# Moving the inputs of the long products off multiples of 32 bytes in a one-layer hybrid decoder kernel

## What is computed

```python
x = x + 0.5 * swiglu(rms_norm(x), ffn1_gate, ffn1_up, ffn1_down)    # 1024 -> 2816 -> 1024
h = rms_norm(x); proj = h @ w_in                                    # 1024 -> 5120
y_a = moba_attention(q, k, v, rel_bias)                             # 8 heads of 64
y_b = rwkv7_time_mix(h, r, k, v, ...)                               # 8 heads of 64, with low-rank products of h
merged = sigmoid(ga) * (y_a @ proj_a) + sigmoid(gb) * (y_b @ proj_b)
x = x + merged @ w_out
x = x + 0.5 * swiglu(rms_norm(x), ffn2_gate, ffn2_up, ffn2_down)
out = rms_norm(x)
```

## Time and profile before

| | us |
|---|---|
| median of 3 runs | 625.43 |
| the three runs | 623.08, 625.43, 632.48 |
| the profiled execution's own time | 623.61 |
| its span, first to last instruction | 621.8 |

### The profile page before, as it was taken

How to read it: one execution, slowest core, us unless ns; L and a number is a source line. 1 busy time by engine, 2 the same in 40 slices (tenths; PEclk the granted TensorE clock), 3 DMA queues, 4 the chain that set the end, 5 groups by cost and what they waited for, 6 DMA issues and landing times.

```text
span 621.8 us, 15455 instructions
## 1 busy us (share of the span) xinstructions
PE 611.3 (98%) x6716; PEld 596.6 (96%) x6716; DVE 419.7 (68%) x491; ACT 296.7 (48%) x345; POOL 91.8 (15%) x92
## 2 busy tenths in 40 slices
PE   8999999999999999999999999999999999999996
PEld 8999999999999999999988899999999999999996
DVE  5866887755656369968993337878667666665663
ACT  6644555443334264535555445545544444443332
POOL 0117700000114000020015423004100000000130
PEclk9999999999999999999999999999999999999999
DMA  8677666656555246685242232356556666556551
GB/s 298 213 245 218 198 202 202 194 173 197 176 188 185 76 136 204 203 177 163 71 137 71 71 105 73 122 183 203 161 177 202 202 186 187 188 169 208 179 167 67
DMA packets 100672, 105.40 MB, mean 170 GB/s; under 512 B 2244, under 2 KB 98732, under 8 KB 100628
## 3 DMA queue, kind: packets, MB, share of 16 engines
q1 hardware_dynamic: 99380, 101.47, 51.1%
q0 software_dynamic: 1088, 3.02, 2.2%
q10 hardware_dynamic: 160, 0.27, 0.1%
HBM read 103.50 MB, written 1.25 MB: 168 GB/s over the span
## 4 chain that ended last, share of the span: by engine, by line
PE 86%; DVE 7%; ACT 3%; DMA 3%; issue 1%; SPq 0%; ACTq 0%; DVEq 0%
PE two L1460 24%; PE two L1461 23%; PE two L1462 23%; PE two L1456 12%; DVE w_lo L904 4%; ACT w_hi L532 2%; DMA w_raw<-in_ffn_down 1%; DMA w_raw<-in_ffn_up 1%; DMA w_raw<-in_ffn_gate 1%; DVE w_lo L914 1%; PE two L1734 1%; PE two L1735 1%; PE two L1736 1%; PE two L1879 0%; DVE hlo_f L923 0%
## 5 line engine op out<-in xcount | busy, mean ns | idle before, releaser
L532 ACT ACTIVATE w_hi<-w_raw 128x2048 fp32r<-128x2048 f32 (+1 forms) x86 | 162.5, 1890 | 241.7 <-PE two L1462 207.7
L904 DVE TENSOR_TENSOR w_lo<-w_raw,w_hi 128x2048 fp32r<-128x2048 f32 (+1 forms) x86 | 199.6, 2321 | 82.7 <-ACT w_hi L532 82.4
L1460 PE MATMUL two<-hlo_f,w_hi 128*128 128x256 f32 x640 | 177.7, 278 | 1.4 <-DVE w_lo L904 1.4
L1461 PE MATMUL two<-hhi_f,w_lo 128*128 128x256 f32 x640 | 177.2, 277 | 0.0
L1462 PE MATMUL two<-hhi_f,w_hi 128*128 128x256 f32 x640 | 177.2, 277 | 0.0
L1460 PEld LDWEIGHTS two<-hlo_f,w_hi 128*128 128x128 f32 x640 | 120.3, 188 | 2.4 <-issue 1.3
L1461 PEld LDWEIGHTS two<-hhi_f,w_lo 128*128 128x128 f32 x640 | 120.2, 188 | 0.0
L1462 PEld LDWEIGHTS two<-hhi_f,w_hi 128*128 128x128 f32 x640 | 120.2, 188 | 0.0
L1460 PE MATMUL two<-hid_lo_t,w_hi 128*128 128x256 f32 x352 | 97.9, 278 | 0.9 <-DVE w_lo L904 0.3
L1461 PE MATMUL two<-hid_hi_t,w_lo 128*128 128x256 f32 x352 | 97.4, 277 | 0.0
L1462 PE MATMUL two<-hid_hi_t,w_hi 128*128 128x256 f32 x352 | 97.4, 277 | 0.0
(11 more groups left out here) (342 smaller groups left out, 984.3 us busy)
## 6 DMA issues: line engine op xcount, KB each, us to landing
w_raw<-in_ffn_up SPq DMA_DIRECT2D x21, 1024.0 KB, 5.3
w_raw<-in_ffn_gate SPq DMA_DIRECT2D x20, 1024.0 KB, 5.3
w_raw<-in_w_in SPq DMA_DIRECT2D x20, 1024.0 KB, 5.1
w_raw<-in_ffn_down SPq DMA_DIRECT2D x16, 896.0 KB, 4.6
w_raw<-in_ffn_down SPq DMA_DIRECT2D x8, 1024.0 KB, 4.9
w_raw<-in_w_out SPq DMA_DIRECT2D x4, 1024.0 KB, 4.9
w_raw<-in_proj_a SPq DMA_DIRECT2D x4, 512.0 KB, 3.6
w_raw<-in_proj_b SPq DMA_DIRECT2D x4, 512.0 KB, 4.2
```

The source lines that it names most:

```text
L532: nc.scalar.activation(whi[slot][:, 0:kts], raw[slot][:, 0:kts], ACT.Copy).then_inc(sg["hi_ready"], 1)
L904: nc.vector.tensor_tensor(wlo[slot][:, 0:kts], raw[slot][:, 0:kts], whi[slot][:, 0:kts].bitcast(F32), ALU.subtract).then_inc(sg["lo_ready" ...
L1460: mm(dst, whi[slot][:, k_, cols], xl, start=start, stop=False)
L1461: mm(dst, wlo[slot][:, k_, cols], xh, start=False, stop=False)
```

## The change

The pairs of tiles `hhi_f`/`hlo_f`, `hid_hi_t`/`hid_lo_t`, `hhi_m`/`hlo_m` and `mhi`/`mlo` each become one tile (`pair_f`, `pair_hid`, `pair_m`, `pair_mg`) that is 8 elements longer, of which a view is taken that begins 4, 4, 2 and 6 elements in, that is 16, 16, 8 and 24 bytes behind a multiple of 32. With the pads, the distance to the weights goes from -64 bytes to -48 for the feed-forward input, -80 for the hidden rows, -56 for the mixing's input and -72 for the merged branches. `yahi`, `yalo`, `ybhi`, `yblo` and all weight tiles stay where they were; the mixing's scratch tiles from `ks` on move by 32 bytes and stay at multiples of 32. No instruction of any engine is added, removed or moved against another, and all shapes stay; operands' addresses differ.

```diff
+        def shifted(name, tiles, by, scope):
+
+            flat = sb(name, [P, 2 * tiles * T + 8], F32R, scope)[:, by:by + 2 * tiles * T]
+            both = flat.rearrange("p (a k t) -> p a k t", a=2, k=tiles)
+            return both[:, 0], both[:, 1]
+
         with ExitStack() as sc:
             h_f = sb("h_f", [P, KD, T], scope=sc)
             sb("pad_f", [P, 48], scope=sc)
-            hhi_f = sb("hhi_f", [P, KD, T], F32R, scope=sc)
-            hlo_f = sb("hlo_f", [P, KD, T], F32R, scope=sc)
+            hhi_f, hlo_f = shifted("pair_f", KD, 4, sc)
             silu = sb("silu", [P, 2, T], scope=sc)
             prod = sb("prod", [P, 2, T], scope=sc)
-            hid_hi = sb("hid_hi_t", [P, FT, T], F32R, scope=sc)
-            hid_lo = sb("hid_lo_t", [P, FT, T], F32R, scope=sc)
+            sb("pad_hid", [P, 48], scope=sc)
+            hid_hi, hid_lo = shifted("pair_hid", FT, 4, sc)
...
-            hhi_m = mb("hhi_m", [P, KD, T], F32R)
-            hlo_m = mb("hlo_m", [P, KD, T], F32R)
+            hhi_m, hlo_m = shifted("pair_m", KD, 2, mix)
...
-                mb("pad_lora", [P, 48], scope=sc)
+                mb("pad_lora", [P, 40], scope=sc)
...
-                mb("pad_y", [P, 32], scope=sc)
+                mb("pad_y", [P, 24], scope=sc)
...
-                mhi = mb("mhi", [P, KD, T], F32R, scope=sc)
-                mlo = mb("mlo", [P, KD, T], F32R, scope=sc)
+                mb("pad_mg", [P, 56], scope=sc)
+                mhi, mlo = shifted("pair_mg", KD, 6, sc)
```

## The result

| | before | after |
|---|---|---|
| median, us | 628.95 (4 runs, 623.08 to 633.35) | 642.85 (4 runs, 641.96 to 643.91) |
| profiled execution's own time, its span | 623.61, 621.8 | 641.96, 640.2 |

The ratio is 1.0266, 95% interval 1.0224 to 1.0307: the changed kernel is slower by 2.7%. The ratio goes by fast runs alone (those not over 1.5% above the fastest of their kernel), so it is not the quotient of the two medians, which is 1.022. The runs before were joined by a fourth, which moved their median from 625.43 to 628.95.

A forecast was written before the change was run, and what follows sets the result against it. The prediction took TensorE's matmul stream to bound the kernel. With 0 us for instructions, writers and each matmul group, the profiled 623.6 us stayed, forecast as 624 us, range 606 to 643.

The forecast's parts named there:

- What bounds the kernel: Whole kernel: TensorE's matmul stream sets the time; 1 ns on the start-to-start time of 4440 matmuls is 4.4 us.
- Two pitches at the same addresses: Long matmuls: start-to-start times of 113.3 and 117.7 ns on the same tiles, the switch coming at a stall.
- the two of 216 and 217: Profile rows of 256 float32 columns, one operand off a multiple of 32: 216 and 217 ns, read as no odd-start cost.
- The term of the sum that was put at 0 us: The matmul stream: 4440 long matmuls keep 113.3 ns and the present share of high pitch, so 0 us for each group.
- The prediction's own sign of being wrong: Feed-forward input and hidden rows: both 16-byte offsets, covering 3168 matmuls, move the pitch over 3 ns in one direction.
- The upper bound: Long matmuls: all that stand low go to 117.7 ns, 15.3 us more, giving 639 us.
- the band from 638 upwards: Whole-kernel time of 638 us and more, from the high pitch everywhere or a worse one: chance 0.18.
- The rival of a lost lower state: Gate and up loops first, then down projection: 113.3 ns no longer reached, 15.3 us more, 639 us; chance 0.18 with worse pitches.
- The writers: ScalarE and VectorE writes to the moved tiles: no added cost, VectorE's hid_lo writes staying at 684 ns.
- The late weights: Down projection: 6.34 us load, then 1.93 and 2.30 us splitting on the chain, taking back part of any gain.
- Load against stream: Long matmuls: the skill's rule of free weight loading gives 0; the two pitches were said to support it only in part.
- A 65th line per row: Mixing's and merged rows, 8 and 24 bytes in: would touch one more 16-byte memory line; no row showed a cost.

The follow-up runs named there:

- the weights-alone run: Only the split weights w_hi and w_lo start 16 bytes further in than in the kernel before; moving rows unchanged, distance -80 bytes: 641.79 us, ratio 1.0231.
- the two traced all-odd kernels at -64: Weights and moving rows all 16 bytes further in than in the kernel before, first without ya and yb (623.58 us), then with them (622.81 us).
- the one at +64: Against the kernel before, all starts 16 bytes behind a multiple of 32, distance +64 except the mixing's input at -64: 633.57 us, ratio 1.0147.

## Why the prediction was wrong

The forecast was 624 us and no change; the kernel took 642.85, just inside the range's upper end of 643, and 2.7% slower.

**What bounds the kernel** was right: from start to start the 4440 matmuls carried 18.0 of the 18.4 us, all long ones 18.2. **Two pitches at the same addresses** was right, but I used it for the size of the loss only. That the share of the upper pitch makes the spread of the runs before, as the prediction allows, is not shown: in the five traced kernels whose moved tiles stand at -64 on multiples of 16, that share goes from 5 to 23% of the long matmuls, the spans only from 621.0 to 622.5 us and not in step with it, and no execution of over 626 us was traced.

**The step that failed** is "Of these the nearest rows are the two of 216 and 217, which see no effect of an odd start, and so I take an unchanged 113.3". In each of those rows one operand starts between multiples of 32 bytes, and no row where neither does stands beside them, so they could not show that an odd start costs nothing. They stream 256 columns in 216 ns, half the rate of the long products, while one load can follow another every 112 ns; that this leaves room in which a collision would not show is my reading, not tested. And they say nothing of the distance. The term of the sum that was put at 0 us measured 18.0. The runs put two things in its place. For the feed-forward input and the hidden rows (3168 matmuls) it is the distance: with the weights moved along, the pitch went back to 113.3. For the mixing's input and the merged rows the start off a multiple of 16 is enough, since it costs 120 ns even at -64; their distances, -56 and -72, changed as well, and what these alone would cost with both operands on a multiple of 16 cannot be had. The prediction's own sign of being wrong came true: both offsets of 16 bytes moved the pitch by more than 3 ns in one direction.

**The upper bound** was 117.7 ns and 639 us; the pitches became 116.7, 119.2 and 120.0. The bound was a pitch of the old distance, and a new distance has pitches of its own. The measured 642.85 us lies in the band from 638 upwards, to which the prediction gave 0.18. The rival of a lost lower state came nearest in time, but not in kind: the argument against it, that four different offsets would all have to hurt, was the wrong way round. Nearly every distance tried hurts: of the ten multiples of 16 in the table, -64 and +64 are the only ones that reached 113.3. Six (-112, -16, +16, +48, +80, +112) were not tried.

**The writers** at nought were right: 686 ns against 684, and ScalarE's hidden-row write at 614 ns in both traces. **The late weights** of the down projection had been named as what would eat part of a gain; they ate part of the loss instead. The chain by line from 130 to 192 us before, and from 134 to 200 us after:

```profile
by line: PE two L1460 22.6%; PE two L1461 21.2%; PE two L1462 21.2%; DVE w_lo L904 17.2%; DMA w_raw<-in_ffn_down 10.2%; ACT w_hi L532 8.7%; issue 0.8%; SPq L334 0.1%; ACTq L531 0.1%; DVEq L903 0.0%
...
by line: PE two L1464 33.2%; PE two L1466 32.9%; PE two L1465 32.6%; PE two L1460 1.6%
```

Load and splitting are gone from it. In time, 1056 matmuls by 119.25 - 113.4 = 5.85 ns are 6.2 us, and the group grew by 4.6: the waits that stood there before shrank by 1.6.

**Load against stream.** The moving rows of the weights-alone run lie as before, and moving only the matrices took 5.5 ns more per matmul (118.8 against 113.3). So the pitch depends on where the one operand lies against the other, which is what one would see if a load and the stream beside it slow each other; which load meets which row was not separated. The Trainium skill (TensorE: Matmul & The Clock Gate, Step-by-step: what each phase is for) says that loading the next weights steals no SBUF bandwidth from the running matmul. This measurement speaks against free overlap for fp32r with 256 moving columns and a load for each matmul, and the measurement decides.

Starts 8 bytes in at an unchanged distance took 120.2 ns, starts 16 or 32 bytes in 113.3 (with stretches of 117.8 for the 32). The Trainium skill (SBUF — State Buffer, Specifications (TRN2)) gives SBUF 16-byte lines. The trace agrees in so far as 8 bytes cost and 16 and 32 do not. A 65th line per row would, by an estimate from that page's line size, lengthen the pitch by 1/64, 1.8 ns, and 6.9 were measured, so it is not the whole of it.

## What stays open

What decides at a stall between 113.3 and 117.8 was not found; the two traced all-odd kernels at -64 took the lower pitch in nearly every stretch (their 22 executions lie between 621.3 and 624.6 us), the one at +64 did not. Nor is it shown why -64 and +64 are the good distances, whether they are good beyond counting modulo 256 in this one layout, or whether a stationary matrix off a multiple of 16 costs anything when the moving row is on one: no distance of 64 can be had with one operand on and the other off.

## What to carry to other kernels

In this kernel, where matmuls with 128-column loads of their own follow one another without gaps, the pitch depended on where the two operands lie against each other in SBUF. The placement that was best here is worth trying first elsewhere: moving rows 64 bytes short of the stationary matrices modulo 256, both at multiples of 16 bytes (64 bytes past them mostly stood at 117.8, 637 us). Check it from start to start in the trace, since a tile added anywhere ahead shifts it. Rows at half the column rate did not show the effect, and bounds from another address pattern did not bound the new one. When a change moves only addresses, move the other operand along as the first experiment: it tells the distance from the start in one run.

## What the runs showed that I had not expected

The stream has repeating patterns with fixed means rather than a smooth cost: 113.3, 116.7, 117.8, 118.3, 119.2 and 120.0 ns among them, held for up to a thousand matmuls. A misplacement of 4 bytes, which also leaves the multiples of 16, costs as much as one of 64 (120 ns at -60 as at 0). One stationary matrix of two out of place slowed all three matmuls of the triple (118.4, 119.2, 115.8 ns). And the common move by 16 bytes narrowed the spread of the runs to 2.5 us, where the kernel before had 10.
